# Memory scales, rotary angles and distances on GpSimd, and mem_2 turned one slab later, in a two-block transformer kernel on Trainium2

## The reference, cut to what matters

```python
def rmsnorm(x, w):
    y = xf * lax.rsqrt(jnp.mean(xf * xf, axis=-1, keepdims=True) + EPS)
    return y * w

def apply_rotary(t, positions):
    half = t.shape[-1] // 2
    inv_freq = ROPE_BASE ** (-jnp.arange(half) / half)
    ang = positions[..., None] * inv_freq
    t1, t2 = t[..., :half], t[..., half:]
    return jnp.concatenate([t1 * cos - t2 * sin, t1 * sin + t2 * cos], axis=-1)

def retention(q, k, v, positions):
    # per chunk of 64 tokens, 8 heads of 32 (q, k) and 64 (v)
    dist = jnp.abs(idx[:, None] - idx[None, :])
    decay_in = jnp.exp(log_g[:, None, None] * dist)
    scores = jnp.einsum('bnihd,bnjhd->bnhij', qc, kc) * decay_in
    y_in = jnp.einsum('bnhij,bnjhe->bnihe', scores, vc)
    ...

def conv_module(a, b, ...):      # gated, 31 taps, causal, 512 channels
    ...

mem_n   = rmsnorm(mem, norm_mem_w)       # 256 rows, keys and values of block 1
m       = rms_norm(mem_2, mem_norm_g_2)  # 256 rows, keys and values of block 2
```

## Time and profile before

| | us |
|---|---|
| median of 3 runs | 946.92 (946.70 to 946.98) |
| the profiled execution | 947.47 |
| its span, first to last instruction | 945.6 |
| TensorE matmul busy | 921.4 |
| VectorE busy | 649.1 |
| ScalarE busy | 475.7 |
| GpSimd busy | 6.9 |

### The profile page before, as it was taken

The page is one execution under the profiler, slowest core; times in us unless marked ns, Lnnn a source line. Parts: engine busy times, 40 slices in busy tenths (PEclk is TensorE's granted clock), DMA queues, the critical chain, the costliest instruction groups (busy, mean ns, idle before and its releaser), DMA issues.

```text
span 945.6 us, 15110 instructions
## 1 busy us (share of the span) xinstructions
PE 921.4 (97%) x6344; PEld 852.7 (90%) x6344; DVE 649.1 (69%) x928; ACT 475.7 (50%) x533; POOL 6.9 (1%) x37
## 2 busy tenths in 40 slices
PE   6998999999999999999999999999999999999996
PEld 6896999889899999999999999999898899999995
DVE  5799999888576555555866886765786765555555
ACT  6686435474464444445646545653564543433332
POOL 1000000000000000000000000000000000000000
PEclk9999999999999999999999999999999999999999
DMA  9665545454345555564755544555453455555551
GB/s 316 239 226 181 178 134 171 142 177 149 119 151 199 185 177 186 199 192 148 232 178 178 161 152 137 177 170 186 134 184 128 134 179 183 188 196 188 178 178 45
DMA packets 112470, 164.48 MB, mean 174 GB/s; under 512 B 2784, under 2 KB 90464, under 8 KB 112416
## 3 DMA queue, kind: packets, MB, share of 16 engines
q1 hardware_dynamic: 111856, 161.87, 52.3%
q0 software_dynamic: 560, 1.84, 0.7%
HBM read 162.64 MB, written 1.05 MB: 173 GB/s over the span
## 4 chain that ended last, share of the span: by engine, by line
PE 87%; DVE 8%; DMA 2%; ACT 1%; issue 1%; SPq 0%; DVEq 0%; ACTq 0%
PE ps L527 27%; PE ps L529 27%; PE ps L528 27%; DVE w_lo L1457 3%; DMA w_ring<-in_w_in 2%; DVE c_acc L1596 2%; PE ps L644 1%; PE ps L555 1%; PE ps L552 1%; PE ps L553 1%; PE ps L680 0%; ACT w_hi L1043 0%; DVE acc L1988 0%; DVE h L1515 0%; DVE mem_l L1472 0%
## 5 line engine op out<-in xcount | busy, mean ns | idle before, releaser
L1457 DVE TENSOR_TENSOR w_lo<-w_ring,w_hi 128x2048 fp32r<-128x2048 f32 x147 | 335.6, 2290 | 144.5 <-ACT w_hi L1043 142.9
L527 PE MATMUL ps<-xh,w_hi 128*128 128x256 f32 x1176 | 335.6, 285 | 8.5 <-DVE w_lo L1552 8.3
L1043 ACT ACTIVATE w_hi<-w_ring 128x2048 fp32r<-128x2048 f32 x147 | 280.0, 1908 | 107.4 <-DMA w_ring<-in_w_in 27.6
L528 PE MATMUL ps<-xl,w_hi 128*128 128x256 f32 x1176 | 333.5, 284 | 0.0
L529 PE MATMUL ps<-xh,w_lo 128*128 128x256 f32 x1176 | 333.4, 283 | 0.0
L527 PEld LDWEIGHTS ps<-xh,w_hi 128*128 128x128 f32 x1176 | 226.3, 192 | 10.8 <-DVE w_lo L1552 8.8
L528 PEld LDWEIGHTS ps<-xl,w_hi 128*128 128x128 f32 x1176 | 226.4, 193 | 0.7
L529 PEld LDWEIGHTS ps<-xh,w_lo 128*128 128x128 f32 x1176 | 226.3, 192 | 0.0
L527 PE MATMUL ps<-w_hi,ff_h 128*128 128x512 f32 x216 | 84.3, 390 | 0.0
L528 PE MATMUL ps<-w_lo,ff_h 128*128 128x512 f32 x216 | 84.2, 390 | 0.0
L529 PE MATMUL ps<-w_hi,ff_l 128*128 128x512 f32 x216 | 84.0, 389 | 0.0
(11 more groups left out here) (296 smaller groups left out, 1158.2 us busy)
## 6 DMA issues: line engine op xcount, KB each, us to landing
w_ring<-in_w_in SPq DMA_DIRECT2D x36, 1024.0 KB, 5.1
w_ring<-in_mlp_up_w SPq DMA_DIRECT2D x16, 1024.0 KB, 5.4
w_ring<-in_mlp_down_w SPq DMA_DIRECT2D x16, 1024.0 KB, 4.9
w_ring<-in_w_gate_ffn SPq DMA_DIRECT2D x11, 1024.0 KB, 5.2
w_ring<-in_w_up_ffn SPq DMA_DIRECT2D x11, 1024.0 KB, 5.3
w_ring<-in_w_down_ffn SPq DMA_DIRECT2D x11, 1024.0 KB, 4.9
w_ring<-in_xkv_w SPq DMA_DIRECT2D x8, 1024.0 KB, 5.4
w_ring<-in_w_out SPq DMA_DIRECT2D x8, 1024.0 KB, 4.9
```

Of the source, the lines that this page charges most:

```text
L527: pe.matmul(o, lh, rh, start=first, stop=False)
L528: pe.matmul(o, lh, rl, start=False, stop=False)
L1043: act.activation(w_hi[:, s, :], w_ring[:, s, :], ACT.Copy).then_inc(hi_done, 1)
L1457: dve.tensor_tensor(w_lo[:, s, :], w_ring[:, s, :], w_hi[:, s, :].bitcast(F32), ALU.subtract).then_inc(lo_done, 1)
```

## The change

- GpSimd gets helpers `after` (a semaphore step behind each instruction) and `memory_scales`: the sums become scales in 14 instructions instead of VectorE's 11, since it has no fused form of three operands here. It computes the rotary angles, then the scales of `mem`, then the distances, and after the mask of `ws_t` the scales of `mem_2`. Its gain and gate loads now wait for the last decay instead of for `rv`, because the longer decay table covers the place of `gain`.
- `mem_2` becomes slab 13 and the third value slab of memory one slab 12; loads, `hi`, `lo` and TensorE's order follow. `mem_2` is turned after the third value slab. Its splits come in two halves with `hi(15)` and `lo(15)` between, and the first two key slabs wait only for the halves of their banks.
- The decay tables get 384 columns, so that a head's decay is one instruction; the rotary products take both halves of the tokens at once, 6 instructions of 128x512 instead of 12 of 128x256.
- The numbers of taps between the steps of VectorE's queue change: 8, 6, 17, 6, 6, 8, 4, 9, 10, 10, 8 become 10, 14, 6, 10, 6, 2, 4, 11, 10, 10, 9; the last two groups stay.

```diff
-I_M2 = 12
-I_V1 = (10, 11, 13, 14)
+I_M2 = 13
+I_V1 = (10, 11, 12, 14)
...
+            def memory_scales(use, r):
+
+                pool.wait_ge(norm_sq, 2 * use + 2)
+                after(pool.tensor_scalar(pv[:, :], sq_sum[:, 2 * use:2 * use + 2], 1.0 / D, EPS, ALU.mult, ALU.add))
+                after(pool.tensor_scalar(r.bitcast(I32), pv[:, :].bitcast(I32), -0.5, RSQRT_MAGIC, ALU.mult, ALU.add))
+                for n in range(3):
+                    after(pool.tensor_tensor(pt[:, :], r, r, ALU.mult))
+                    after(pool.tensor_tensor(pt[:, :], pt[:, :], pv[:, :], ALU.mult))
+                    after(pool.tensor_scalar(pt[:, :], pt[:, :], -0.5, 1.5, ALU.mult, ALU.add))
+                    ins = pool.tensor_tensor(r, pt[:, :], r, ALU.mult)
+                    if n < 2:
+                        after(ins)
+                ins.then_inc(mem_scales, 1)
...
+            pool.wait_ge(ang_ready, 1)
+            memory_scales(Q_MEM, r_mem)
+            pool.wait_ge(mem_scales, 1)
+            after(pool.tensor_copy(dist[:, 0:S], dist_i[:, :]))
...
+            pool.tensor_copy(dist[:, S:S + P], dist[:, 0:P]).then_inc(dist_set, 1)
+
+            pool.wait_ge(dist_set, 1)
             pool.wait_ge(const_ready, 4)
             pool.wait_ge(ws_loaded, 16)
             pool.memset(ws_t[CHUNK:P, :, 0:CHUNK], 0.0).then_inc(ws_masked, 1)

             pool.wait_ge(ws_masked, 1)
-            pool.wait_ge(rv_ready, 2)
+            memory_scales(Q_MEM2, r_mem2)
+            pool.wait_ge(mem_scales, 2)
+            pool.wait_ge(s_dec_ready, RET_HEADS)
             load_gain(G_F)
...
             for j in range(4):
                 pe.wait_ge(norm_lo, 2 * j + 2)
                 form_b_rows(I_V1[j], 2 * j, m_t, (0, 1), j == 0, j == 3).then_inc(slab_used, 1)
-                if j == 1:
+                if j == 2:
                     pe.wait_ge(rg_in, 2)
                     normed(N_MEM)
                     memory_transpose(N_MEM2, w_ring[:, PLACE[I_M2], :].rearrange("p (t n) -> p t n", n=D), range(4))
...
-                if i == I_K1:
-                    normed(N_MEM2)
+                if i in (I_K1, I_K1 + 1):
+                    pe.wait_ge(norm_lo, KD * (N_MEM2 + 1) - (6, 4)[i - I_K1])
...
             gate_silu(0)
+            hi(12)
+            gate_silu(1)
             mem2_tok = w_ring[:, PLACE[I_M2], :].rearrange("p (t n) -> p t n", n=D)
             act.wait_ge(w_loaded[PLACE[I_M2]], 16 * (USES[I_M2] + 1 + (PLACE[I_M2] == 0)))
             for tb in range(TB):
                 norm_square(mem2_tok, tb, Q_MEM2, mem2_sq[:, tb, :])
-            gate_silu(1)
-            hi(13)
+            hi(14)
             memory_rows(N_MEM2, mem2_tok, r_mem2)
-            hi(14)
             act.wait_ge(norm_sq, 2 * Q_MEM2 + 2)
-            memory_split_hi(N_MEM2, mem2_h)
+            memory_split_hi(N_MEM2, mem2_h, range(4))
             hi(15)
+            memory_split_hi(N_MEM2, mem2_h, range(4, KD))
             hi(16)
...
-            token_scales(Q_MEM, r_mem)
-            dve.sem_inc(mem_scales, 1)
             lo(6)
-            conv(8)
+            conv(10)
...
-                dve.scalar_tensor_tensor(s_dec[:, hd % 2, 0:S], tok(hd % 4)[:, 0:S], sc, dec[:, hd, :], ALU.mult, ALU.mult)
-                after(dve.scalar_tensor_tensor(s_dec[:, hd % 2, S:S + P], tok(hd % 4)[:, S:S + P], sc, dec[:, hd, 0:P], ALU.mult, ALU.mult))
-                dve.sem_inc(s_dec_ready, 1)
+                dve.scalar_tensor_tensor(s_dec[:, hd % 2, :], tok(hd % 4)[:, 0:RET_COLS], sc, dec[:, hd, :], ALU.mult, ALU.mult).then_inc(s_dec_ready, 1)
...
             lo(11)
             conv(6)
             scaled_gate_ret(1)
-            token_scales(Q_MEM2, r_mem2)
-            dve.sem_inc(mem_scales, 1)
+            lo(12)
+            conv(10)
+            lo(14)
             conv(6)
-            lo(13)
-            conv(8)
-            lo(14)
-            memory_split_lo(N_MEM2, mem2_h, mem2_l)
+            memory_split_lo(N_MEM2, mem2_h, mem2_l, range(4))
+            conv(2)
             lo(15)
+            memory_split_lo(N_MEM2, mem2_h, mem2_l, range(4, KD))
             lo(16)
             conv(4)
```

More of the change, by code:

```diff
@@ L282, in build @@
                at("yc_l", [P, 4, S], split0 + 3 * D, F32R)]
+        pv, pt = new("pv", [P, TB]), new("pt", [P, TB])
         used = [0]
@@ L403, in _ @@
             for j in range(4):
-                if j == 2:
+                if j == 3:
                     load(I_M2, a["mem_2"].rearrange("a (t p) d -> p (a t) d", p=P))
@@ L503, in _, with after @@
                                pattern=[[1, P]], channel_multiplier=-1).then_inc(const_ready, 1)
+            count = [0]
+            def after(ins):
+                count[0] += 1
+                ins.then_inc(pool_step, 1)
+                pool.wait_ge(pool_step, count[0])
+            def memory_scales(use, r):
[10 more added lines that the diff above has]
+                ins.then_inc(mem_scales, 1)
@@ new lines, in _ @@
+            pool.wait_ge(pos_loaded, 16)
+            pool.wait_ge(tables_ready, 1 + ROPE_HALF)
+            after(pool.tensor_copy(pos_f[:, :], pos_i[:, :]))
+            sin_a, cos_a = ang[:, 0, :, :], ang[:, 1, :, :]
+            shape = [P, TB, ROPE_HALF]
+            after(pool.tensor_tensor(sin_a, pos_f[:, :].unsqueeze(2).broadcast_to(shape), freq[:, :].unsqueeze(1).broadcast_to(shape), ALU.mult))
+            after(pool.tensor_scalar(turns[:, :, :], sin_a, 1.0 / (2 * PI), ROUND, ALU.mult, ALU.add))
@@ new lines, in _ @@
+            after(pool.tensor_scalar(turns[:, :, :], turns[:, :, :], ROUND, None, ALU.subtract))
+            for part in (TWO_PI_A, TWO_PI_B, TWO_PI_C):
+                after(pool.tensor_scalar(cos_a, turns[:, :, :], -part, None, ALU.mult))
+                after(pool.tensor_tensor(sin_a, cos_a, sin_a, ALU.add))
+            after(pool.tensor_scalar(sin_a, sin_a, SIN_MAX, -SIN_MAX, ALU.min, ALU.max))
+            after(pool.tensor_scalar(cos_a, sin_a, 0.0, 2.0, ALU.max, ALU.mult))
+            after(pool.tensor_tensor(cos_a, cos_a, sin_a, ALU.subtract))
@@ new lines, in _ @@
+            pool.tensor_scalar(cos_a, cos_a, -1.0, PI / 2, ALU.mult, ALU.add).then_inc(ang_ready, 1)
+            pool.wait_ge(ang_ready, 1)
+            memory_scales(Q_MEM, r_mem)
+            pool.wait_ge(mem_scales, 1)
+            after(pool.tensor_copy(dist[:, 0:S], dist_i[:, :]))
+            after(pool.tensor_scalar(dist[:, S:S + P], dist[:, 0:P], 0.0, 2.0, ALU.max, ALU.mult))
+            after(pool.tensor_tensor(dist[:, 0:P], dist[:, S:S + P], dist[:, 0:P], ALU.subtract))
+            after(pool.memset(dist[CHUNK:P, 0:CHUNK], FAR))
@@ L767, in ret_values @@
             def ret_values(hd):
+                if hd == 0:
+                    normed(N_MEM2)
                 pe.wait_ge(s_dec_ready, hd + 1)
@@ L1625, in _ @@
             dve.tensor_tensor(both, both, cols_g[:, KD * C_F:KD * (C_F + 1)], ALU.mult).then_inc(gain_product, 1)
[L1626 to L1629, removed]
             memory_split_lo(N_MEM, mem_h, mem_l, range(4))
@@ L1632, in _ @@
             dve.wait_ge(qk_ready, 2)
[L1633 to L1644, removed]
+            shape = [P, TB, 2 * RET_HEADS, ROPE_HALF]
+            view = qk[:, :, :].rearrange("p t (g e f) -> p t g e f", e=2, f=ROPE_HALF)
+            res = qkr[:, :, :].rearrange("p t (g e f) -> p t g e f", e=2, f=ROPE_HALF)
+            t = [rope_t[:, j, :, :].rearrange("p t (g f) -> p t g f", f=ROPE_HALF) for j in range(4)]
+            sin, cos = (sincos[:, e, :, :].unsqueeze(2).broadcast_to(shape) for e in range(2))
+            dve.tensor_tensor(t[0], view[:, :, :, 0, :], cos, ALU.mult)
+            dve.tensor_tensor(t[1], view[:, :, :, 1, :], sin, ALU.mult)
+            dve.tensor_tensor(t[2], view[:, :, :, 0, :], sin, ALU.mult)
+            after(dve.tensor_tensor(t[3], view[:, :, :, 1, :], cos, ALU.mult))
+            dve.tensor_tensor(res[:, :, :, 0, :], t[0], t[1], ALU.subtract)
+            after(dve.tensor_tensor(res[:, :, :, 1, :], t[2], t[3], ALU.add))
+            dve.sem_inc(rope_ready, 2)
             lo(9)
             memory_split_lo(N_MEM, mem_h, mem_l, range(4, KD))
-            conv(6)
             lo(10)
-            conv(17)
+            conv(14)
             def ret_decay(hd):
@@ L1696, in _ @@
                 lo(18 + j)
-                conv((9, 10, 10, 8)[j])
+                conv((11, 10, 10, 9)[j])
             k_lo(0)
```

7 lines of the change are left out of this document (4 added, 3 removed).

## The result

| | kernel before | changed kernel |
|---|---|---|
| median us | 947.12 (6 runs, 946.70 to 947.41) | 950.54 (6 runs, 950.25 to 951.39) |
| profiled execution us | 947.47 | 950.45 |
| span us | 945.6 | 948.7 |
| mean granted TensorE clock | 0.998 | 0.995 |

The changed kernel takes 1.0039 of the time of the kernel before (95% interval 1.0029 to 1.0048): 3.4 us slower, where 2.5 us less were forecast. The busy line of the page answers the earlier trace rows.

A forecast was written before the change was run, and what follows sets the result against it. TensorE, busy 97% of 945.6 us, bounds the kernel. Gaps -5.3 plus stalls 1.2 and 1.6 give -2.5; 947.47 - 2.5 - 0.55 (profiled execution over median) = 944.4 us; range 941.3 to 950.8.

The forecast's parts named there:

- the ceiling: 5.3 us, the most the change can bring, since it takes no matmul away from TensorE.
- Four gaps: TensorE's waits: slab 6 0.81, slab 11 1.93, scaled mem_2 rows 1.98, slab 13 about 0.6 us.
- Slab 6: TensorE's wait at 44.99 for the slab's low half; its 0.81 us goes with rotary angles and scales off VectorE.
- slab 11: TensorE's 1.93 us wait at 76.48; goes by moving nine taps behind it, with 0.8 us to spare.
- The first chain: Scales of mem on GpSimd: 14 steps of 0.42, 5.9 us from 40.6; TensorE stalls 1.2 us before slab 7.
- The second chain: Scales of mem_2 on GpSimd: fourteen steps from 81.6 to 87.5; stall of 1.6 us where 1.98 stood.
- GpSimd's holds: GpSimd steps delay VectorE some 0.1 us each, harmless since VectorE stands behind ScalarE anyway in both stretches.
- the select of 0.66 at 20.42: GpSimd row, twin 0.29, beside a VectorE subtraction ending 20.93; it follows a DMA issue; called unable to decide.
- the two rivals with a hold: Rival 1 (chance 0.25) and rival 2 (0.30): VectorE's instructions with two SBUF inputs make GpSimd's reads wait.
- rival 2: Conv steps hold GpSimd too: stalls 4.0 and 4.6, +3.3, 950.2 us; sign: both chains over 15 us; chance 0.30.
- the forecast's own range: 941.6 to 946.5 us, from no stalls to stalls of 2.2 and 2.7 with 0.5 us a step.
- Rival 1: Only the long subtractions hold GpSimd's reads: stalls 3.3 and 3.7, +1.7, 948.6 us; chance 0.25.

The follow-up runs named there:

- e1: The changed kernel with both chains of memory scales (of mem and mem_2) back on VectorE; 942.37 us, 0.9952 of the kernel before.
- e8: The kernel of e1 measured once more, in another call; 942.67 us, 0.9954 of the kernel before.
- e9: As e8, with rotary angles and distances back on VectorE too, so GpSimd has no chain; 943.66 us, 0.9965 of the kernel before.
- e2: The changed kernel with only the second chain (scales of mem_2) back on VectorE; 944.99 us, 0.9976 of the kernel before.
- e3: The changed kernel, but the ten taps beside the second GpSimd chain read one SBUF tile instead of two; 945.79 us, 0.9989 of the kernel before.
- e4: The changed kernel with the ten taps beside the second chain moved behind slab 14's subtraction and among the key slabs; 946.06 us, 0.999 of the kernel before.
- e6: The changed kernel with one GpSimd memset, which only writes, ahead of the second chain; 950.43 us.
- e7: The changed kernel with two GpSimd memsets ahead of the second chain; 951.64 us.
- e5: The changed kernel with only the first chain (scales of mem) back on VectorE; 948.95 us, 1.0014 of the kernel before.
- e11: The changed kernel with four two-column GpSimd copies ahead of the second chain, started when the second gate is there; 949.43 us, 1.0025 of the kernel before.

## Why the prediction was wrong

**What bounds, and the ceiling: right.** Four gaps of 5.3 us in all. With the scales on VectorE nearly all of it comes back and nothing else is late (4.9 us in e1, 4.3 in e8).

**Slab 6 and slab 11: the gaps are gone, as put.** For slab 6 the reason isn't shown. In e9 its subtraction stands behind the same 21 small instructions as in the kernel before (the angles are ten, not eleven), and TensorE doesn't wait: it asks 0.32 later (45.54 against 45.22) and the subtraction starts 0.49 earlier (43.19 against 43.68), which is the whole gap of 0.81. So that gap belonged in part to how the profiled execution of the kernel before had started. The taps that leave were counted in two ways, 2.8 us (seven) for slab 11 and 3.6 (nine) for the second gate. Nine is right for both, since the two that are added stand where VectorE idles, ahead of slab 7's subtraction; slab 11 had 0.8 more to spare than was put.

**The first chain: the stall right, by two errors that cancel.** The step was put at 0.42; it is 0.28 on a quiet VectorE. The nearest row had 0.24 between end and start at the beginning of the program; between two steps of the chain it is 0.08. But one step is held 2.1 us and those beside taps are 0.32 to 0.40, so the chain takes 6.3 us where 5.9 stood, and the stall is 1.22 where 1.2 stood. Other traces have 1.0 to 1.8, so the agreement is luck twice over. Its true price is 2.6 us (e2 against e1): I had not followed the slide of ScalarE and VectorE to the keys, where 0.84 is lost when nothing else stops TensorE. The prediction had given that stretch nothing.

**The second chain: the step that failed.** The forecast took 14 steps of 0.42 beside a VectorE in full work, 5.9 us, and a stall of 1.6. It is 9.4 and 5.3, since VectorE's instructions hold GpSimd's: under *GpSimd's holds* the prediction priced only the other direction, and let nothing hold GpSimd. The choice behind it was to read the select of 0.66 at 20.42 as the effect of a DMA issue rather than of the subtraction beside it; the row ended 0.15 us behind the subtraction, and the other reading had no number at all. The prediction gave the two rivals with a hold 0.55 together, and put its number on the side with 0.45. e3 and e4 show which it is: with no second SBUF input beside it, or with no VectorE beside it, the first step is 0.19. A read that follows no DMA issue shows the same: the first instruction of the angles ends 0.04 or 0.05 us behind a subtraction in all eleven traces that have it on GpSimd. It takes 0.22 in the changed kernel, where it starts at 26.12 and the subtraction ends at 26.30, and 0.38 to 1.19 in the others, where it starts earlier. VectorE and GpSimd in e1:

```profile
23.75 2.29 DVE L1507 TENSOR_TENSOR w_lo<-w_ring,w_hi 128x2048 fp32r<-128x2048 f32 x1 [0.60 <-ACT w_hi L1092]
```
```profile
25.24 0.85 POOL L531 CAST pos_f<-pos_i 128x2 f32<-128x2 int32 x1 [4.39 <-DMA pos_i<-in_positions]
```

**The rivals.** The time lies near the upper end of the stated range, which rival 2 had set; the forecast's own range ended at 946.5. Rival 2 gave 950.2, and 950.54 was measured; its direction, its mark (the two chains over 15 us together; they take 15.7) and its mechanism, both kinds of instruction holding GpSimd, were right. Its parts were not: stalls of 4.0 and 4.6 where 1.2 and 5.3 are. It let the first chain crawl through taps at 0.5 a step, which is 0.40, and began with too few steps done when slab 6's subtraction came (seven, not four). For the second chain it expected a slot between every two taps, and there was none for the first step. And it had no term for the clock. So the sum agreed in part by chance. Rival 1 is nearest to e4, 946.06, 2.5 us lower than its 948.6, mostly since the step is 0.28.

**A term that stood in no sum: TensorE's clock.** The transposes behind the long stall and what follows run slower. Two-microsecond stretches of the changed kernel, and then of e4, with its stall of 1.8. The columns are the stretch, its length, busy time and count of instructions (of TensorE, its weight loads, VectorE, ScalarE and GpSimd in the first block, of TensorE alone in the second), then the granted clock, the DMA share and GB/s:

```profile
92.00:94.00 2.00, 0.00 (x0) 0.00 (x0) 0.00 (x0) 1.91 (x2) 0.00 (x0) 0.85 0.85 298
94.00:96.00 2.00, 1.95 (x9) 1.98 (x10) 0.00 (x0) 0.76 (x2) 0.00 (x0) 0.50 0.01 2
96.00:98.00 2.00, 2.00 (x12) 1.87 (x12) 1.89 (x5) 2.00 (x4) 0.00 (x0) 0.80 0.00 0
```
```profile
88.00:90.00 2.00, 0.18 (x1) 1.00 0.31 56
90.00:92.00 2.00, 1.99 (x17) 1.00 0.99 323
92.00:94.00 2.00, 2.00 (x10) 1.00 0.79 209
```

In the changed kernel the granted clock is 0.85, 0.50 and 0.80 of full speed in the three stretches; in e4 it stays at 1.00. Half of full speed is the lower of the two levels, 1.2 GHz. From the first transpose to the first scores of the retention heads behind the first key slab, e3 takes 103.34 - 90.26 = 13.08 us at full clock and the changed kernel 108.46 - 94.05 = 14.41: 1.3 us. Thus the forecast of -2.5 and the +3.1 in the trace differ by 3.7 (second stall), 1.3 (clock), and 0.75 (a later start, which is no part of the change), less 0.1.

## What to carry to other kernels

In this kernel small dependent chains go to GpSimd without harm only where VectorE is idle, or works from one SBUF tile (e3), for the whole chain. One step beside an instruction with one input from PSUM wasn't held either: the third of the distances in e1, 0.46 us at 33.87, between two that were held. Elsewhere, beside back-to-back instructions with two SBUF inputs, price each meeting with a long one at that one's full length, and a fresh start in a stretch of short ones at what is left of the stretch, and of a long one that follows it at once (e6, e7). Price the moved chain by who waits for it, not by what it frees: here it freed about 4.5 us (two chains of 2.3) of an engine that had room and lengthened the path of the one that hadn't. When one row of the trace fits a hold and the other reading has no number, the sum belongs on the hold.

## What the runs showed of the hardware that I had not expected

- A dependent two-column step on GpSimd takes 0.28 us from start to start, of which 0.19 is the instruction; VectorE's is 0.20. A chain of 14 alone would be 3.9 us by that, an estimate, since every chain here meets a subtraction.
- GpSimd steps that are going when a stretch of taps begins get in at each tap, 0.40 apart; a reading step that comes fresh into the stretch was shut out for 3.16, 3.17, 5.21 and 5.05 us in four kernels, while memsets of the same size took 0.10 or 0.11 beside it. VectorE's own taps show no delay from the two-column steps that do get in (ten taps take 4.03 to 4.05 us either way). The wider steps of the distances do delay them: eight taps take 3.42 us beside the first of these in the changed kernel and 3.25 in e1, which has none there.
- Stalls of TensorE of 1.8 and 2.2 us left its clock at full speed; after those of 3.7 to 5.4 us it was granted half. The loss isn't in proportion to the stall. From the first transpose to the first key scores, where e3 takes 13.08 at full clock, e5 (stall 4.1) takes 107.18 - 91.26 = 15.9, e11 (stall 3.7) 108.39 - 92.80 = 15.6 and the changed kernel (stall 5.1) 14.4, so a shorter stall cost up to 1.5 us more clock; e6 and e7, with 5.4 both, take 14.9 and 15.7. That is most of why e5 and e11 returned less than their shorter stalls had gained.
